# Second layer's input projections: from float32 products to three float32r products each

## Chip, cores and metric

One core of one Trainium2 chip. The metric is device time in microseconds of one execution, the median of several runs.

## What is computed

Two blocks of two layers each over 512 tokens of width 1024, in float32. The change touches the second layer of the first block, a gated linear recurrence (`c_layer` of the reference) over the 512 tokens and 256 context tokens:

```
q, zf, zb, i, g = split_cols(modulate(x, shift, scale) @ w_in, widths)
zfc, zbc, ic    = split_cols(hc @ w_in[:, C_F_WIDTH:3 * C_F_WIDTH + C_I_WIDTH], ...)
q = silu(q) * 128 ** -0.5          # 8 heads, key width 128
o_f = scan(q, i, zf), o_b = scan(q, i, zb, reversed)     # each starts from the context's state
y = rmsnorm(o_f + o_b) * g_norm * silu(g) @ w_out
x_new = layer_norm(DEEPNORM_ALPHA * x + gate * y)
```

`w_in` is 1024 x 5120. Those products with `w_in` are the input projections meant in the title.

## The kernel before

The kernel is one program per engine: PE (matmul), ACT, DVE, POOL and SP (which starts the weight loads), written out in order and joined by semaphores. Weights come in chunks of 1024 x 256 (1 MB) into three slots `WR`, used in turn; SP (L1391 on) loads chunk n once the last product of chunk n-3 has been done.

**Two ways to multiply.** Most stages split a float32 chunk into a high part (`hi`, float32r, one copy by ACT or DVE) and a low part (`lo`, the difference, one subtraction by POOL at L3011, written over the raw chunk), split the activations alike, and sum three float32r matmuls per 128 rows of the contraction: hi by hi, hi by lo, lo by hi (`split_f`, L698 to L700). The second layer's input projections multiply the raw float32 chunk by the float32 rows `HT` (`product_half`, L989, L993, L998). One such matmul stands in the trace as two instructions.

**Order of the second layer.** The projections are cut into units, each of two halves that fill one of two PSUM banks (`obank`): for every head `z` has three units (forward 512 columns, backward 512 columns, context 2 x 256), for every pair of heads `q` has two of 512 columns and `i` three of 2 x 256, and `g` has four keys of two units of 2 x 256. A first stretch makes z, q, i for the first head or pair. Then follow eight steps (`STEPS`, st = 0 to 7), one per head. In each, PE forms seven levels of attention inside blocks of 128 tokens (`levels(st, 0)` to `(st, 6)`, L1013, written `lv0` to `lv6` below) plus the chunk states, and the units needed next are put between them by hand: `c_slots` gives the number of halves in each of eight places, `between(0)` to `between(7)`. Steps 0, 2, 4 carry z of the next head and q of the next pair (5 units), steps 1, 3, 5 z and i (6 units), step 6 z and three units of g, step 7 the last five units of g.

**What a level needs.** POOL forms the arguments (`level_args`, L2998 to L3000, two level buffers `HW`, so level g waits for the matmuls of level g-2), ACT takes the exponential (`level_exp`, L1673), DVE multiplies by keys and queries (`level_operand`, L2304 and L2305), PE multiplies, DVE merges the result (`level_scores`, L2326).

**What the next step needs.** When `between(2)` has ended the third unit of z of the next head, ACT empties it (L1624) and makes keys (L1655), an exponential (L1641), the exponential for level 5, a logarithm (L1647) and the exponential for level 6, with table loads between. After the logarithm DVE runs `log_f_and_sums` (L2267, four scans L2273 to L2276, three small operations L2278 to L2280, of which L2279 reads two operands in SBUF) and signals `hg_sums`. From this wait ACT's `state_factors` (L1660 to L1669), DVE's `state_operands` (L2286) behind them, with which PE starts the next step (transposes, L1084), and POOL's arguments of the next step's first level. DVE's order is: operand 5, `log_f_and_sums`, scores 4, operand 6, scores 5, `state_operands`, scores 6.

**After the steps.** Heads are normed on DVE (L2392), turned on PE (L1049), split into hi by ACT (L1693) and lo by DVE (L2399), and multiplied by `w_out` as three float32r products (L638 to L640). ACT's order there is: hi of the first chunk `y10.0` (L1429), then hi of the heads.

The rows x stay in SBUF (`X`, L2546 adds the result to them). The tables (`TAB`) hold masks for the attention of the first and third layers.

Of the kernel before, what the change touches and what calls it, by code (L numbers as in the profile page):

```python
# [15 lines left out]
F32 = mybir.dt.float32  # L16
U32 = mybir.dt.uint32
I32 = mybir.dt.int32
ALU = mybir.AluOpType
# [29 lines left out]
def table_layout():  # L49

    sizes = [("ident", P), ("ones", P), ("pick", 2), ("win_lo", P), ("win_hi", P), ("dil", 1280),
             ("lv", P * len(LEVELS)), ("rot_ax", P), ("rot_pt", P),
             ("cos_ax", L), ("sin_ax", L), ("chunk", L), ("cols", 6)]
    at, out = 0, {}
    for name, n in sizes:
        out[name] = (at, at + n)
        at += n
    return out, at


def make_tables():
# [9 lines left out]
    put("pick", i[:, None] % 32 == np.arange(2)[None, :])  # L71
# [53 lines left out]
def program(nc, a, out, stop=99):  # L125
    lay, tw = table_layout()
    ctx = ExitStack()
    with ctx:
# [55 lines left out]
        chunks = []  # L184
# [18 lines left out]
        TAB_FIRST = lay["pick"][1]  # L203
# [5 lines left out]
        PICK = tab("pick")  # L209
# [14 lines left out]
        HKS = view(w + 19456, L, name="h_keys")  # L224
# [3 lines left out]
        HO = view(hi_at, TL, D, name="h_out")  # L228
# [9 lines left out]
        def c_slots(st):  # L238
# [8 lines left out]
            if st == LAST:  # L247
                share = (2, 2, 2, 2, 2, 0, 0, 0)
# [63 lines left out]
        Y_HI, Y_LO = parts("ab_out_hi", ht_at, KD, LT), parts("ab_out_lo", w + 4608, KD, LT)  # L312
        C_HI = parts("c_out_hi", w + 4096, KD, L)
# [224 lines left out]
        def _(pe):  # L538
# [10 lines left out]

            def chunk(pieces, kt=KD):  # L550

                n = len(chunks)
                s = n % WSLOTS
                chunks.append((pieces, kt))
                wcount[s] += 16 * len(pieces)
                pe.wait_ge(wload[s], wcount[s])
                return WR[:, s]
# [31 lines left out]
            def split_chunk(name, pieces, kt=KD, by="a"):  # L589
# [5 lines left out]
                w_hi, w_lo = OWN_HI[name] if name in OWN_HI else W_HI[:, len(splits) % 2], W_LO[n % WSLOTS]  # L595
# [4 lines left out]
                splits.append((n % WSLOTS, kt, w_hi, wload[n % WSLOTS], wcount[n % WSLOTS], by, hi_done, len(hi_list)))  # L600
# [365 lines left out]
            c_weights, c_release = {}, {}  # L966
# [6 lines left out]
            def product_half(unit, half):  # L973

                kind, key, part = unit
                if half == 0:
                    if part == 0:
                        c_weights[kind, key] = chunk(c_pieces(kind, key))
                        c_release[kind, key] = len(released)
                        released.append((None, 0))  # L980
# [4 lines left out]
                wv = c_weights[kind, key]  # L985
                ps = obank[n % 2]
                if kind in "zq" and part < 2:
# [3 lines left out]
                elif kind == "z":  # L991
                    for k in range(KD):
                        last = pe.matmul(ps[:, half * LC:(half + 1) * LC], wv[:, k, half * P:(half + 1) * P], HT[:, k, L:LT],  # L993
                                         start=k == 0, stop=k == KD - 1)
# [2166 lines left out]
```

## Time and profile before

| | |
|---|---|
| median of 3 runs | 2315.05 us (2310.82 to 2320.57) |
| profiled execution, its own time | 2313.38 us |
| its span, first to last instruction | 2311.5 us |
| mean granted clock of TensorE | 0.974 |
| PE busy | 2140.4 us (93%) |
| DVE busy | 1055.3 us (46%) |
| POOL busy | 807.8 us (35%) |
| ACT busy | 668.6 us (29%) |

PE is TensorE's matmul queue, ACT ScalarE, DVE VectorE, POOL GpSimd, SP the queue that issues loads. A timeline row gives the start and the duration in us, engine, source line, operation, output and inputs with shape, the number of instructions merged, and in brackets the idle time before it and what ended it. Matmuls overlap, so their pace is read from one start to the next and not from the duration. The granted clock is a share of TensorE's full speed.

### The profile page before, as it was taken

Reading aid. Unit: us, or ns where it says so; the run is one execution under the profiler, and the core shown is the slowest. Engines: PE = TensorE matmul, PEld = TensorE weight load, DVE = VectorE, ACT = ScalarE, POOL = GpSimd, SP = SyncE. Lnnn points to the kernel's source line nnn. Section 1 sums busy time; section 2 is a strip of 40 time slices with the busy share of each in tenths; the row PEclk is TensorE's granted clock in tenths of the full one; section 3 lists DMA queues with packets and bytes.
Section 4 is the critical chain, followed back from the end, with each engine's and each line's share of the span. In section 5 each row is a group of like instructions: output and inputs, shape, how many; then the busy total and the mean of one; then the engine's idle time right before and its main releaser. Section 6 shows DMA issues by size and latency. Waiting matters only on the chain. (4 is left out here: it accounts for less than half of the span.)

```text
span 2311.5 us, 27285 instructions
## 1 busy us (share of the span) xinstructions
PE 2140.4 (93%) x11287; PEld 1710.3 (74%) x11287; DVE 1055.3 (46%) x1685; ACT 668.6 (29%) x1043; POOL 807.8 (35%) x429
## 2 busy tenths in 40 slices
PE   4999988989999999987998889999998999999998
PEld 3887767867575767876756678888887688888886
DVE  1113674663566555559985651111126674111114
ACT  3223323324545454632102441000013443100011
POOL 1421113411333333328200025554544234554553
PEclk7999999989999999998999999999999999999999
DMA  9233123533111111121111122322322222322322
GB/s 295 69 110 97 40 71 92 128 110 91 37 37 37 37 37 37 55 82 60 37 55 37 56 73 74 109 91 91 106 79 90 91 91 74 109 91 91 106 86 82
DMA packets 183114, 187.41 MB, mean 81 GB/s; under 512 B 25728, under 2 KB 162256, under 8 KB 182864
## 3 DMA queue, kind: packets, MB, share of 16 engines
q1 hardware_dynamic: 173040, 175.42, 24.6%
q10 hardware_dynamic: 9376, 8.16, 1.3%
q8 instruction: 90, 1.47, 0.3%
q0 software_dynamic: 576, 2.10, 0.2%
q14 instruction: 32, 0.26, 0.0%
HBM read 183.56 MB, written 2.10 MB: 80 GB/s over the span
## 5 line engine op out<-in xcount | busy, mean ns | idle before, releaser
L3011 POOL TENSOR_TENSOR weights_lo<-weights_raw,weights_hi 128x2048 fp32r<-128x2048 f32 (+1 forms) x101 | 456.8, 4523 | 863.6 <-ACT weights_hi L1429 667.5
L698 PE MATMUL ring<-input_hi,weights_hi 128*128 128x512 f32 x784 | 305.5, 390 | 4.1 <-POOL weights_lo L3011 3.9
L700 PE MATMUL ring<-input_hi,weights_lo 128*128 128x512 f32 x784 | 305.1, 389 | 0.0
L699 PE MATMUL ring<-input_lo,weights_hi 128*128 128x512 f32 x784 | 305.1, 389 | 0.0
L2837 DVE CAST weights_hi<-weights_raw 128x2048 fp32r<-128x2048 f32 (+1 forms) x72 | 87.6, 1217 | 366.2 <-PE ring L700 173.9
L2998 POOL TENSOR_TENSOR h_w<-h_p 128x512 f32<-128x512 f32 x56 | 77.1, 1377 | 356.0 <-PE ring L1013 239.1
L989 PE MATMUL obank<-acts,weights_raw 128*128 128x512 f32 x384 | 175.6, 611 | 0.0
L698 PEld LDWEIGHTS ring<-input_hi,weights_hi 128*128 128x128 f32 x784 | 147.1, 188 | 36.2 <-issue 5.8
L699 PEld LDWEIGHTS ring<-input_lo,weights_hi 128*128 128x128 f32 x784 | 147.2, 188 | 30.6
L700 PEld LDWEIGHTS ring<-input_hi,weights_lo 128*128 128x128 f32 x784 | 147.2, 188 | 30.4
L998 PE MATMUL obank<-weights_raw,acts 128*128 128x256 f32 x640 | 142.1, 380 | 0.0
L1347 PE MATMUL ring<-weights_lo,hidden_hi 128*128 128x512 f32 x352 | 137.0, 389 | 0.0
L1348 PE MATMUL ring<-weights_hi,hidden_lo 128*128 128x512 f32 x352 | 137.0, 389 | 0.0
L1346 PE MATMUL ring<-weights_hi,hidden_hi 128*128 128x512 f32 x352 | 136.9, 389 | 0.0
L989 PEld LDWEIGHTS obank<-acts,weights_raw 128*128 128x128 f32 x384 | 73.8, 198 | 84.8 <-issue 84.7
L998 PEld LDWEIGHTS obank<-weights_raw,acts 128*128 128x128 f32 x640 | 119.9, 190 | 16.1 <-issue 0.8
L2858 DVE TENSOR_TENSOR f_gate<-f_gate,ring 128x1024 f32<-128x1024 f32 x22 | 26.9, 1221 | 212.4 <-PE ring L700 212.4
L3114 POOL TENSOR_TENSOR hidden_lo<-f_gate,hidden_hi 128x1024 fp32r<-128x1024 f32 x22 | 52.6, 2391 | 162.3 <-ACT hidden_hi L1925 162.3
L1925 ACT ACTIVATE hidden_hi<-f_gate 128x1024 fp32r<-128x1024 f32 x22 | 23.4, 1063 | 246.8 <-DVE f_gate L2858 246.8
L1429 ACT ACTIVATE weights_hi<-weights_raw 128x2048 fp32r<-128x2048 f32 x32 | 61.2, 1912 | 96.0 <-DMA weights_raw<-in_w_in_ab 53.3
L698 PE MATMUL ring<-ab_in_hi,weights_hi 128*128 128x512 f32 (+1 forms) x224 | 77.7, 347 | 10.4 <-POOL ab_in_lo L3017 10.4
L1013 PEld LDWEIGHTS ring<-h_w 128*128 128x128 f32 x448 | 58.4, 199 | 37.0 <-DVE h_w L2305 31.2
(465 smaller groups left out, 4391.0 us busy)
## 6 DMA issues: line engine op xcount, KB each, us to landing
weights_raw<-in_w_ada SPq DMA_DIRECT2D x24, 1024.0 KB, 5.3
weights_raw<-in_ffn_w_gate SPq DMA_DIRECT2D x22, 1024.0 KB, 5.4
weights_raw<-in_ffn_w_up SPq DMA_DIRECT2D x22, 1024.0 KB, 5.3
weights_raw<-in_ffn_w_down SPq DMA_DIRECT2D x16, 1024.0 KB, 5.0
weights_raw<-in_w_in_c SPq DMA_DIRECT2D x12, 1024.0 KB, 5.2
weights_raw<-in_w_in_ab SPq DMA_DIRECT2D x9, 1024.0 KB, 7.8
weights_raw<-in_w_in_c SPq DMA_DIRECT2D x16, 512.0 KB, 5.3
weights_raw<-in_ev_w_in SPq DMA_DIRECT2D x8, 1024.0 KB, 5.5
```

What stands on the lines that cost most here:

```text
L698: pe.matmul(o, hi[:, k, ms], xh[:, k, t0:t0 + n], start=k == 0, stop=False)
L699: pe.matmul(o, hi[:, k, ms], xl[:, k, t0:t0 + n], start=False, stop=False)
L700: last = pe.matmul(o, lo[:, k, ms], xh[:, k, t0:t0 + n], start=False, stop=k == KD - 1)
L989: last = pe.matmul(ps[:, 0:L], wv[:, k, part * P:(part + 1) * P], HT[:, k, 0:L], start=k == 0, stop=k == KD - 1)
L998: last = pe.matmul(ps[:, half * WC:(half + 1) * WC], HT[:, k, t * P:(t + 1) * P], wv[:, k, :], start=k == 0, stop=k == KD - 1)
L1346: pe.matmul(o, F_HI[f // 2][:, f % 2, ts], hi[:, k, :], start=f == 0, stop=False, skip_group_check=True)
L1347: pe.matmul(o, F_HI[f // 2][:, f % 2, ts], lo[:, k, :], start=False, stop=False, skip_group_check=True)
L1348: last = pe.matmul(o, F_LO[f // 2][:, f % 2, ts], hi[:, k, :], start=False, stop=end, skip_group_check=True)
L1429: act.activation(w_hi[:, 0:kt, :], WR[:, slot, 0:kt, :], ACT.Copy).then_inc(done, 1)
L2837: dve.tensor_copy(w_hi[:, 0:kt, :], WR[:, slot, 0:kt, :]).then_inc(done, 1)
L2998: pool.tensor_tensor(w4[:, :, :, 0, :], refs.to_broadcast([P, 2, n, h2]), p4[:, :, :, 0, :], ALU.subtract)
L3011: pool.tensor_tensor(W_LO[slot][:, 0:kt, :], WR[:, slot, 0:kt, :], w_hi[:, 0:kt, :], ALU.subtract).then_inc(sem("w_lo"), 1)
```

## The change

All of z, q, i, g but the first head's z and the first pair's q become three float32r products. Split are i0, then in pairs (z1, q1), (z2, i1), (z3, q2), (z4, i2), (z5, q3), (z6, i3), (z7, g0), then g1, g2, g3: 18 chunks (`C_SPLIT`). Chunks of even index use one raw slot, of odd index another; the third slot holds the high part of the odd ones. So a slot is loaded again only when all products of its chunk are done. ACT makes each high part (`c_weights_hi`) and POOL each low part (`c_weights_lo`), in steps 0 to 6 after level 3's and after level 6's work, in step 7 after level 2's and level 5's. The rows' high parts go where `X` and some tables were, so `X` is written to DRAM from POOL's queue and read back by SP behind the second chunk of the output product; the table for the third layer's attention is loaded later by ACT's queue. DVE makes the six high parts of the rows before `abs_z(0)` and two low parts after `log_f_and_sums(0)`, POOL the other low parts, the context's when (z, 0, 2) is done. The order of i0's three units changes. In step 7 the halves move from (2, 2, 2, 2, 2, 0, 0, 0) to (1, 1, 2, 2, 2, 2, 0, 0). `levels(st, 1)` stands ahead of the state sums before and after.

```
+        X_KEPT = nc.dram_tensor("x_kept", (TL, P, D), F32).ap()
+        x_back_after = []
...
-                share = (2, 2, 2, 2, 2, 0, 0, 0)
+                share = (1, 1, 2, 2, 2, 2, 0, 0)
...
+        C_XH, C_XH2 = parts("c_in_hi", x_at, TL, KD, P), parts("c_in_hi_ctx", own_at, 2, KD, P)
+        C_XL = parts("c_in_lo", ht_at, KD, LT)
+        C_SPLIT = [("i", 0)]
+        for hb, j in STEPS[:-1]:
+            C_SPLIT += [("z", HH * hb + j + 1), ("iq"[j == 0], hb + 1) if hb + 1 < HEADS // HH else ("g", 0)]
+        C_SPLIT = C_SPLIT[:15] + [("g", 1), ("g", 2), ("g", 3)]
...
+        def c_hi_homes(i):
+
+            if i % 2:
+                return [(0, KD, C_IN_WR[c_wr_slot[0]])]
+            return C_LATE if i >= 12 else [(0, KD, C_IN_HO)]
...
+            def c_ready(kind, key):
+
+                if (kind, key) not in C_SPLIT:
+                    c_reserve(kind, key)
+                    n = c_chunk[kind, key]
+                    pe.wait_ge(wload[slot_of[n]], arrival[n])
+                    c_raw[kind, key] = WR[:, slot_of[n]]
+                    return
+                i = C_SPLIT.index((kind, key))
+                if i:
+                    c_reserve(kind, key, slot_of[c_chunk["i", 0]] if i % 2 == 0 else c_odd_slot[0])
+                if (kind, key) == ("g", 3):
+                    holder[c_wr_slot[0]] = c_chunk["g", 3]
+                    x_back_after.append(len(chunks) + 1)
+                pe.wait_ge(sem("c_w_hi"), c_parts_made(i))
+                pe.wait_ge(sem("c_w_lo"), c_parts_made(i))
+                c_raw[kind, key] = None
...
-                if kind in "zq" and part < 2:
+                if wv is None:
+                    last = split_half(unit, half, ps)
...
+            def split_half(unit, half, ps):
+
+                kind, key, part = unit
+                i = C_SPLIT.index((kind, key))
+                lo = W_LO[slot_of[c_chunk[kind, key]]]
+                if kind in "zq" and part < 2:
+                    for k in range(KD // 2 * half, KD // 2 * (half + 1)):
+                        ms = slice(part * P, (part + 1) * P)
+                        pe.matmul(ps[:, 0:L], c_hi(i, k)[:, ms], C_XH[:, :, k, :], start=k == 0, stop=False)
+                        pe.matmul(ps[:, 0:L], c_hi(i, k)[:, ms], C_XL[:, k, 0:L], start=False, stop=False)
+                        last = pe.matmul(ps[:, 0:L], lo[:, k, ms], C_XH[:, :, k, :], start=False, stop=k == KD - 1)
+                elif kind == "z":
+                    o, ms = ps[:, half * LC:(half + 1) * LC], slice(half * P, (half + 1) * P)
+                    for k in range(KD):
+                        pe.matmul(o, c_hi(i, k)[:, ms], C_XH2[:, :, k, :], start=k == 0, stop=False)
+                        pe.matmul(o, c_hi(i, k)[:, ms], C_XL[:, k, L:LT], start=False, stop=False)
+                        last = pe.matmul(o, lo[:, k, ms], C_XH2[:, :, k, :], start=False, stop=k == KD - 1)
+                else:
+                    t = 2 * part + half
+                    o = ps[:, half * WC:(half + 1) * WC]
+                    for k in range(KD):
+                        pe.matmul(o, c_x_hi(t, k), c_hi(i, k), start=k == 0, stop=False)
+                        pe.matmul(o, c_x_hi(t, k), lo[:, k, :], start=False, stop=False)
+                        last = pe.matmul(o, C_XL[:, k, t * P:(t + 1) * P], c_hi(i, k), start=False, stop=k == KD - 1)
+                return last
...
+            pe.wait_ge(sem("c_in_lo"), 1)
+            product(("i", 0, 2))
+            c_odd_slot = [slot_of[-1]]
+            mod_next(15)
+            c_wr_slot.append(slot_of[-1])
+            c_before.append(len(chunks) - 1)
+            pe.wait_ge(sem("c_in_lo_v"), 2)
             product(("i", 0, 0))
-            mod_next(15)
+            pe.wait_ge(sem("c_in_lo"), 3)
             product(("i", 0, 1))
-            product(("i", 0, 2))
...
+                if held_before[n] is not None:
+                    sp.wait_ge(*released[held_before[n]])
...
+                if n == x_back_after[0]:
+                    for t in range(TL):
+                        sp.wait_ge(sem(f"x_kept{t}"), 16)
+                        sp.dma_start(X[:, t, :], X_KEPT[t]).then_inc(sem(f"x_back{t}"), 16)
...
+            def c_weights_hi(i):
+
+                n = c_chunk[C_SPLIT[i]]
+                for before in (c_before[:2], c_before[2:])[i] if i < 2 else (c_chunk[C_SPLIT[i - 2]],):
+                    act.wait_ge(*released[before])
+                act.wait_ge(wload[slot_of[n]], arrival[n])
+                for k0, k1, home in c_hi_homes(i):
+                    act.activation(home[:, :, :], WR[:, slot_of[n], k0:k1, :], ACT.Copy).then_inc(sem("c_w_hi"), 1)
...
             h1_tile(5)
+            c_weights_hi(0)
...
             mod_next(14)
+            take_product(("i", 0, 2))
+            mod_next(15)
+            state_factors(0)
+            c_weights_hi(1)
             take_product(("i", 0, 0))
-            state_factors(0)
             level_exp(0)
             level_exp(1)
-            mod_next(15)
             take_product(("i", 0, 1))
-            take_product(("i", 0, 2))
             mod_columns(1, 11)
...
                 level_exp(7 * st + 2)
+                if not more:
+                    c_weights_hi(2 * st + 2)
                 between(0)
                 if st == LAST:
                     s5_row_loads()
                 level_exp(7 * st + 3)
+                if more:
+                    c_weights_hi(2 * st + 2)
                 between(1)
...
                 level_exp(7 * st + 5)
                 if more:
                     log1p(st + 1)
+                else:
+                    c_weights_hi(2 * st + 3)
                 between(3)
                 level_exp(7 * st + 6)
+                if more:
+                    c_weights_hi(2 * st + 3)
                 between(4)
                 if more:
                     state_factors(st + 1)
...
+            act.dma_start(TAB[:, DIL:tw], a["tables"][:, DIL:tw]).then_inc(sem("dil_in"), 16)
...
+            for t in range(6):
+                if t < TL:
+                    dve.wait_ge(sem(f"x_kept{t}"), 16)
+                dve.wait_ge(*read_of(f"h1.{t}"))
+                home = C_XH[:, t] if t < TL else C_XH2[:, t - TL]
+                dve.tensor_copy(home, HT[:, :, t * P:(t + 1) * P]).then_inc(sem("c_in_hi"), 1)
+
+            def c_in_lo(t):
+
+                dve.wait_ge(*product_filled(("q", 0, 1)))
+                ts = slice(t * P, (t + 1) * P)
+                dve.tensor_tensor(C_XL[:, :, ts], HT[:, :, ts], C_XH[:, t], ALU.subtract).then_inc(sem("c_in_lo_v"), 1)
...
             log_f_and_sums(0)
+            c_in_lo(0)
+            c_in_lo(1)
             state_operands(0)
...
+                if c == 0:
+                    dve.wait_ge(sem(f"x_back{t}"), 16)
...
+            def c_weights_lo(i):
+
+                s = slot_of[c_chunk[C_SPLIT[i]]]
+                pool.wait_ge(sem("c_w_hi"), c_parts_made(i))
+                for k0, k1, home in c_hi_homes(i):
+                    pool.tensor_tensor(W_LO[s][:, k0:k1, :], WR[:, s, k0:k1, :], home[:, :, :], ALU.subtract).then_inc(sem("c_w_lo"), 1)
+
             if stop >= 2:
+                for t in range(TL):
+                    pool.wait_ge(sem("x1_ready"), t + 1)
+                    pool.dma_start(X_KEPT[t], X[:, t, :]).then_inc(sem(f"x_kept{t}"), 16)
+                c_weights_lo(0)
+                pool.wait_ge(sem("c_in_hi"), 6)
+                pool.wait_ge(*product_filled(("z", 0, 2)))
+                in_tiles = lambda v: v.rearrange("p k (t c) -> p t k c", c=P)
+                pool.tensor_tensor(in_tiles(C_XL[:, :, L:LT]), in_tiles(HT[:, :, L:LT]), C_XH2[:, :, :, :], ALU.subtract).then_inc(sem("c_in_lo"), 1)
+                pool.wait_ge(*product_filled(("q", 0, 1)))
+                for t in (2, 3):
+                    ts = slice(t * P, (t + 1) * P)
+                    pool.tensor_tensor(C_XL[:, :, ts], HT[:, :, ts], C_XH[:, t], ALU.subtract).then_inc(sem("c_in_lo"), 1)
                 pool.wait_ge(sem("hg_sums"), 1)
                 level_args(0)
                 level_args(1)
+                c_weights_lo(1)
                 for st in range(len(STEPS)):
                     more = st + 1 < len(STEPS)
                     for i in range(2, 7):
                         level_args(7 * st + i)
+                        if i == (3 if more else 2):
+                            c_weights_lo(2 * st + 2)
+                        if i == (6 if more else 5):
+                            c_weights_lo(2 * st + 3)
                     if st == LAST:
                         lo_upto("y10.0")
                     if more:
```

## Rows read from the trace of the kernel before

**Rows 1.** Page: busy times, two groups with mean ns, one DMA issue with us to landing

```profile
PE 2140.4 (93%) x11287; PEld 1710.3 (74%) x11287; DVE 1055.3 (46%) x1685; ACT 668.6 (29%) x1043; POOL 807.8 (35%) x429
...
L3011 POOL TENSOR_TENSOR weights_lo<-weights_raw,weights_hi 128x2048 fp32r<-128x2048 f32 (+1 forms) x101 | 456.8, 4523 | 863.6 <-ACT weights_hi L1429 667.5
...
L1429 ACT ACTIVATE weights_hi<-weights_raw 128x2048 fp32r<-128x2048 f32 x32 | 61.2, 1912 | 96.0 <-DMA weights_raw<-in_w_in_ab 53.3
...
weights_raw<-in_w_in_c SPq DMA_DIRECT2D x12, 1024.0 KB, 5.2
```

**Rows 2.** Timeline of PE, first layer: start us, us, instruction

```profile
99.73 0.39 PE L700 MATMUL ring<-ab_in_hi,weights_lo 128*128 128x512 f32 x1
...
106.08 0.28 PE L698 MATMUL ring<-ab_in_hi,weights_hi 128*128 128x256 f32 x1
...
107.03 0.28 PE L700 MATMUL ring<-ab_in_hi,weights_lo 128*128 128x256 f32 x1
```

**Rows 3.** Timeline of PE, step 3 of the second layer

```profile
745.03 7.03 PE L989 MATMUL obank<-acts,weights_raw 128*128 128x512 f32 x16
751.90 1.05 PE L1013 MATMUL ring<-h_w 128*128 128x128 f32 x8
752.79 7.07 PE L993 MATMUL obank<-acts,weights_raw 128*128 128x256 f32 x32
759.70 1.05 PE L1013 MATMUL ring<-h_w 128*128 128x128 f32 x8
...
778.54 1.16 PE L1013 MATMUL ring<-h_w 128*128 128x128 f32 x8 [1.12 <-DVE h_w L2305]
...
787.54 1.06 PE L1013 MATMUL ring<-h_w 128*128 128x128 f32 x8
```

**Rows 4.** Timeline of PE, step 4

```profile
816.86 1.05 PE L1013 MATMUL ring<-h_w 128*128 128x128 f32 x8
...
826.52 2.08 PE L1013 MATMUL ring<-h_w 128*128 128x128 f32 x8 [3.31 <-DVE h_w L2305]
828.39 8.62 PE L989 MATMUL obank<-acts,weights_raw 128*128 128x512 f32 x16
836.84 1.05 PE L1013 MATMUL ring<-h_w 128*128 128x128 f32 x8
...
843.13 1.16 PE L1013 MATMUL ring<-h_w 128*128 128x128 f32 x8 [0.70 <-DVE h_w L2305]
```

**Rows 5.** Table by stretches, six us of step 4 (granted clock before the DMA share)

```profile
826.00:832.00 6.00, 5.48 (x13) 3.41 (x14) 5.25 (x6) 3.48 (x3) 0.00 (x0) 0.54 0.00 0
```

**Rows 6.** Timeline of ACT, step 3

```profile
768.40 1.58 ACT L1647 ACTIVATE h_t<-h_t,tables 128x1536 f32<-128x1536 f32 x1
...
771.29 1.06 ACT L1673 ACTIVATE h_w<-h_w 128x1024 f32<-128x1024 f32 x1
```

**Rows 7.** Timeline of DVE, step 3

```profile
774.64 0.66 DVE L2276 TENSOR_TENSOR_SCAN h_p<-h_t,tables 128x255 f32<-128x255 f32 x1
...
775.42 0.16 DVE L2279 TENSOR_TENSOR small<-h_p,h_t 128x6 f32<-128x6 f32 x1
```

**Rows 8.** Timeline of DVE, last mixer: two scans over the same size

```profile
1855.63 1.23 DVE L2960 TENSOR_TENSOR_SCAN r_xc<-r_a,r_gi 128x512 f32<-128x512 f32 x1
...
1857.62 5.50 DVE L2960 TENSOR_TENSOR_SCAN r_xc<-r_a,r_gi 128x512 f32<-128x512 f32 x1
```

**Rows 9.** Timeline of POOL in the same stretch

```profile
1857.26 4.77 POOL L3011 TENSOR_TENSOR weights_lo<-weights_raw,weights_hi 128x2048 fp32r<-128x2048 f32 x1 [19.64 <-ACT weights_hi L1429]
```

**Rows 10.** Timeline of DVE, after the second layer's steps

```profile
1042.41 4.58 DVE L2470 SCALAR_TENSOR_TENSOR s_par<-s_par 128x16 f32<-128x16 f32 x1
```

**Rows 11.** Timeline of DVE, start of the second layer

```profile
529.34 1.76 DVE L2260 SCALAR_TENSOR_TENSOR h_t<-h_z 128x1536 f32<-128x1536 f32 x1 [12.63 <-ACT h_z L1624]
```

**Rows 12.** Timeline of PE, end of the second layer

```profile
1005.42 1.10 PE L1049 MATMUL ring<-tables,h_out 128*128 128x128 f32 x8
...
1018.28 0.77 PE L638 MATMUL ring<-c_weights_hi,c_out_hi 128*128 128x512 f32 x1 [1.08 <-DVE c_out_lo L2399]
```

More of the change, by code:

```diff
@@ L548, in take, with reserve, chunk @@
                 return ring[n % 3]
-            def chunk(pieces, kt=KD):
+            def reserve(pieces, kt=KD, slot=None):
                 n = len(chunks)
-                s = n % WSLOTS
+                s = next_slot[0] if slot is None else slot
+                next_slot[0] = (s + 1) % WSLOTS
                 chunks.append((pieces, kt))
                 wcount[s] += 16 * len(pieces)
-                pe.wait_ge(wload[s], wcount[s])
-                return WR[:, s]
+                slot_of.append(s)
+                arrival.append(wcount[s])
+                held_before.append(holder.get(s))
+                holder[s] = n
+                return n
+            def chunk(pieces, kt=KD):
+                n = reserve(pieces, kt)
+                pe.wait_ge(wload[slot_of[n]], arrival[n])
+                return WR[:, slot_of[n]]
             def used_with_unit():
@@ L976, in product_half @@
                 if half == 0:
[L977 to L980, printed above, removed]
+                    if (kind, key) not in c_raw:
+                        c_ready(kind, key)
                     n = products[unit] = len(products)
@@ L984, in product_half @@
                 n = products[unit]
-                wv = c_weights[kind, key]
+                wv = c_raw[kind, key]
                 ps = obank[n % 2]
-                if kind in "zq" and part < 2:
+                if wv is None:
+                    last = split_half(unit, half, ps)
+                elif part < 2:
                     for k in range(KD // 2 * half, KD // 2 * (half + 1)):
@@ L990, in product_half @@
                                          start=k == 0, stop=k == KD - 1)
-                elif kind == "z":
+                else:
                     for k in range(KD):
                         last = pe.matmul(ps[:, half * LC:(half + 1) * LC], wv[:, k, half * P:(half + 1) * P], HT[:, k, L:LT],
-                                         start=k == 0, stop=k == KD - 1)
-                else:
-                    t = 2 * part + half
-                    for k in range(KD):
-                        last = pe.matmul(ps[:, half * WC:(half + 1) * WC], HT[:, k, t * P:(t + 1) * P], wv[:, k, :],
                                          start=k == 0, stop=k == KD - 1)
@@ L1002, in product_half @@
                 last.then_inc(sem("products_filled"), 1)
-                if part == C_PARTS[kind] - 1:
+                c_left[kind, key] -= 1
+                if c_left[kind, key] == 0:
                     released[c_release[kind, key]] = (sem("products_filled"), n + 1)
+            def split_half(unit, half, ps):
[22 more added lines that the diff above has]
+                return last
             def levels(st, i):
```

65 lines of the change are left out of this document (42 added, 23 removed).

## Prediction

> **What bounds the kernel now.** I read the busy shares first: PE works 2140 of 2311.5 us [rows 1]. In the changed stretch, from the first projections to the output product at 1018.28, I then read PE's timeline step by step. PE runs almost without a gap up to T, the end of the third unit of z, at which level 3 starts (759.70 in step 3, 816.86 in step 4) [rows 3, 4]. After T a chain on ACT and DVE paces it: level 6 starts at T + 18.84 in step 3 after 1.12 us of waiting; in step 4 PE waits 3.31 us before level 5 [rows 3, 4]. That chain runs from T through ACT's logarithm, done at 769.98, to DVE's scans [rows 6, 7]. So PE is the bound before T, and a second chain is within 1 to 4 us of it behind T.
>
> **What the products save.** In the first layer 28 float32r matmuls of 512 columns start in 106.08 - 99.73 = 6.35 us, 0.227 each, and 8 of 256 columns in 0.95 us, 0.119 each [rows 2]. A unit of 512 columns takes 751.90 - 745.03 = 6.87 us now and 24 x 0.227 = 5.44 then; a unit of 2 x 256 takes 6.91 and 48 x 0.119 = 5.70 [rows 3]. That is 1.43 and 1.21 us less. Split are 14 + 6 = 20 units of the first kind (z, q) and 7 + 12 + 8 = 27 of the second (z context, i, g): 28.6 + 32.7 = 61 us of PE's time. Were PE the bound throughout, the execution would take 2313.4 - 61 = 2252 us.
>
> The Trainium skill (FP8 and Floating Point Precision, TensorE Precision Notes) says that true FP32 takes four passes through the array. Read with one pass per float32r product, it would save a quarter of the 324 us of these units, 81 us, and end at 2232 us. The starts above give 61, and I use them.
>
> **What splitting costs, where it is covered.** Each of 18 chunks costs ACT 1.91 us and POOL 4.52 us (group means) [rows 1]. The first pair of a step comes between the work of levels 3 and 4. Its slot was free since the end of the step before, loads land after 5.2 us [rows 1], and the product wants it only behind level 3. ACT idles there. I cost it at nothing; its cover is the two z units on PE, and if it went, up to 4.5 us per step would show. The second pair is the z chunk of the next step, whose slot is freed at T. The load lands about T + 6, ACT copies it after the exponential for level 6, at 771.29 + 1.06 = T + 12.65 [rows 6], so until T + 14.6, and then POOL subtracts until about T + 19.5. PE wants it after the next level 0: no wait by itself.
>
> **What POOL's subtraction does to DVE.** This is the step that decides. A scan on DVE issued 0.36 us after such a subtraction of 4.77 us took 5.50 us, and 1.23 us when free; it ended only after the subtraction [rows 8, 9]. Even an operation of 16 columns took 4.58 us [rows 10]. DVE operations with two operands in SBUF stop for the whole of POOL's instruction. In step 3 the fourth scan starts at 774.64 = T + 14.94 and L2279, also with two operands in SBUF, at 775.42 [rows 7]. The new subtraction asks at T + 14.6, while the third scan runs, and is next. Were it 0.5 us later the fourth scan would pass and L2279 would be held, so small shifts don't help. `hg_sums` moves by what is left of the subtraction, about 4.4 us. Queued behind it on DVE are operand 6 and `state_operands`, on ACT `state_factors`, on POOL the next arguments. Late next is PE's level 6 and level 0 of the next step.
>
> The Trainium skill (SBUF — State Buffer, Who interferes with whom) has the rule: a DVE instruction with two SBUF inputs contends with a GpSimd one that reads SBUF, and the later one fully blocks. The trace agrees, 5.50 against 1.23 us.
>
> **The steps.** Before T each of steps 0 to 6 saves 2 x 1.43 + 1.21 = 4.07 us. After T:
> - Steps with q (three): level 0 of the next step starts at T + 26.27 now (843.13), bound by DVE [rows 4]. With the chain 4.4 later it starts at T + 30.7. Net +0.3.
> - Steps with i or g (four): level 6 starts at T + 18.84 + 4.4 = 23.2. PE has then waited about 7 us. After 3.31 us of waiting in step 4 the granted clock was 0.54, half speed, 1.2 GHz [rows 5]; level 5 took 2.08 for 1.05 and the units 8.62 for 7.03, a loss of 2.6 us [rows 4]. Level 6 (1.0), one unit (5.70), the transposes (1.1) and 2.6 make T + 33.6 against T + 27.84 now [rows 3]. Net 5.8 - 4.1 = +1.7.
>
> Sum of the steps: 0.9 + 6.8 = +8 us. Without the clock it would be 0.9 - 4 x 0.9 = -3.
>
> **The start.** The context's low part starts on POOL when (z, 0, 2) ends, 0.8 us before `abs_z(0)` starts now [rows 11], and holds it 3.7 us; I let half reach the chain, since the keys fill part of it on ACT. Two more POOL parts and DVE's own two (1.2 us each, from 1.76 for 1536 columns [rows 11]) stand before i0's latent units, so PE waits some 5 us and loses clock. Less 3 x 1.21 saved: I take +5. Bounds: -4 (all covered) and +9 (nothing). DVE's six high parts (0.6 to 1.2 us each) lie in 12.63 us of idle time [rows 11]; writing and reading x (4 x 0.5 MB each way) lies beside other work, at most +2. The reordered tables and the late table load: 0, covered by the whole layer in between.
>
> **Step 7 and the output product.** Five units save 6.1 us. But g3's slot is freed only with g1, and its high and low part follow level 5's exponential and arguments: about 4 us of waiting and 2.6 of clock, so 0. The chunk y10.0 gets the third slot only after g's last product, just ahead of the first turn of heads. Load 5.2, copy 1.9, subtraction 4.5: 11.6 [rows 1]. Today 12.9 us lie between that turn and the product (1005.42 to 1018.28) [rows 12]. But ACT's copies of the heads are queued behind y10.0's copy, and the norm of the third pair on DVE (two operands in SBUF) waits for the subtraction's end; behind it come 2.2 us of norm, the turn and the split, some 19 us. I take +6; bounds 0 and +9.
>
> **Sum.** 8 + 5 + 0 + 6 = +19 against this execution's own 2313.4: 2332. The median of the runs shown lies 1.7 us above it, so 2334 us.
>
> **Rivals.**
> - *The hold misses the chain.* If DVE gets `hg_sums` out before POOL's subtraction, the steps keep nearly all of 4.1 us: about 3 x 4.1 + 4 x 3.5 = 26 us less, with the start and the end still +3: 2292. For it: ACT's copy could wait for a late load. Against: rows 7, 8 and 10, and a load of 5.2 us where 12 are there. With nothing held at the ends either, 2284. Chance 0.20.
> - *PE stays the bound throughout*, the full count: 2254 with the median's offset. Against: PE waits for DVE already. Chance 0.03.
> - *It cancels.* The chain is late as I say, but PE's clock stays up or half of the hold is covered: steps -3, start +2, end +3: 2317. Chance 0.22.
> - *Slower*, my forecast: its mechanism is the port held from T + 14.6, its price 4.4 us per step, and it decides once that exceeds the 4.07 saved before T. Chance 0.55; its own range is 2327 to 2352.
>
> A difference of 0.5%, 11.6 us, is about what can be told from none here. Chances: faster 0.23, same 0.22, slower 0.55. The range, 2286 to 2350, takes in the first and third rival and the bounds.
>
> **What would show it.** Fourth scan or L2279 at 4 to 5 us in each of seven steps; level 6 at about T + 23; units of z at 5.44 us; a granted clock near 0.5 behind level 6; `y10.0`'s subtraction ending after the turns. If the scans keep 0.66 us and level 6 stays at T + 19, the forecast is wrong.

## The result, and the profile after

The changed kernel takes 2338.0 us (2335.4 to 2338.3, three runs) against 2315.05: a ratio of 1.0093, 95% interval 1.0066 to 1.0121. It is slower, by 23 us; 2334 was forecast. The mean granted clock of TensorE is 0.962, and the span of the profiled execution 2336.2 us, 24.7 more than before.

The page after, to be read against [rows 1]: busy shares, then one group of instructions (busy us, mean ns | idle before, releaser).

```profile
PE 2100.3 (90%) x11879; PEld 1751.5 (75%) x11879; DVE 1134.2 (49%) x1693; ACT 699.0 (30%) x1062; POOL 920.6 (39%) x457
...
L1103 PE MATMUL ring<-h_w 128*128 128x128 f32 x448 | 70.9, 308 | 67.3 <-DVE h_w L2438 67.3
```

PE is busy 40 us less than before, yet the span is longer. GpSimd's subtractions in the other stages keep their mean of 4.52 us. The second row says where the time went: PE waits 67.3 us for `h_w`, the operands of the levels that DVE writes. The same group had 23.0 us before.

PE's timeline in step 3, then in step 4, against [rows 3] and [rows 4]. T is the second row of the first fence and the first of the second.

```profile
742.30 1.16 PE L1103 MATMUL ring<-h_w 128*128 128x128 f32 x8 [0.29 <-DVE h_w L2438]
...
767.77 1.06 PE L1103 MATMUL ring<-h_w 128*128 128x128 f32 x8
...
790.92 2.07 PE L1103 MATMUL ring<-h_w 128*128 128x128 f32 x8 [6.58 <-DVE h_w L2438]
...
800.13 1.06 PE L1103 MATMUL ring<-h_w 128*128 128x128 f32 x8
```

```profile
825.51 1.06 PE L1103 MATMUL ring<-h_w 128*128 128x128 f32 x8
...
848.68 2.08 PE L1103 MATMUL ring<-h_w 128*128 128x128 f32 x8 [5.35 <-DVE h_w L2438]
...
856.11 1.16 PE L1103 MATMUL ring<-h_w 128*128 128x128 f32 x8 [0.82 <-DVE h_w L2438]
```

In step 3 level 6 starts at 790.92 = T + 23.15 (before T + 18.84), behind 6.58 us of idle time, takes 2.07 us instead of 1.16, and level 0 of the next step starts at T + 32.36 (before T + 27.84). In step 4 it is T + 23.17 and T + 30.60 (before T + 20.0 and T + 26.27).

Who is late is on DVE; its rows of step 3, which answer to [rows 7], then POOL's in the same stretch:

```profile
781.61 1.19 DVE L2408 TENSOR_TENSOR_SCAN h_p<-h_t,tables 128x511 f32<-128x511 f32 x1
782.73 4.96 DVE L2409 TENSOR_TENSOR_SCAN h_p<-h_t,tables 128x255 f32<-128x255 f32 x1
...
788.00 0.17 DVE L2413 COPY small<-small 128x12 f32<-128x12 f32 x1
...
789.77 1.09 DVE L2438 TENSOR_TENSOR h_w<-h_w,h_q 128x512 f32<-128x512 f32 x1
```

```profile
782.32 4.82 POOL L3172 TENSOR_TENSOR weights_lo<-weights_raw,c_w_hi 128x2048 fp32r<-128x2048 f32 x1 [5.48 <-ACT c_w_hi L1745]
```

The third scan takes 1.19 us. The fourth, over 255 columns, starts 0.41 us after POOL's subtraction (L3172) and ends 0.55 us after it: 4.96 us against 0.66. It is so in each of steps 0 to 6 (4.95 to 5.00 us). The state sums (L2413) and with them ACT's `small` (L1770, which waited 5.49 us for them) and DVE's operands of level 6 (L2438) come that much later.

The clock in the 3.2 us behind that wait, by stretches (duration, then busy us and instructions of PE, PEld, DVE, ACT, POOL, the granted clock, DMA share, GB/s):

```profile
790.90:794.10 3.20, 3.18 (x15) 3.18 (x16) 1.98 (x2) 3.12 (x8) 1.47 (x2) 0.51 0.00 0
```

0.51 is the lower of the clock's two levels, 1.2 GHz; PE had been idle for 6.58 us.

Where the 24.7 us of span lie, by marks on PE in both traces:

| stretch | before | after | difference | forecast |
|---|---|---|---|---|
| first instruction to z's first product | 497.90 | 502.66 | +4.8 | 0 |
| z's first product to level 0 of step 0 | 64.89 | 68.20 | +3.3 | +5 |
| steps 0 to 6, level 0 to T, sum | 204.43 | 178.36 | -26.1 | -28.5 |
| steps 0 to 6, T to next level 0, sum | 190.22 | 224.33 | +34.1 | +36.5 |
| level 0 of step 7 to its level 6 | 48.91 | 53.35 | +4.4 | 0 |
| level 6 of step 7 to first output product | 11.93 | 18.17 | +6.2 | +6 |
| rest | | | -2.1 | 0 |

The first row can't be told from scatter, and I don't count it as the change's: the two kernels of the experiments that have the first layer of the kernel before start z's first product at 497.48 and 503.44, and those with that of the changed kernel at 500.61 to 506.94. The two rows of step 7 together are +10.7, 60.84 us before and 71.52 after.

### The profile page after: what moved, and what is told of

It reads as the page before. It is cut to its first block and busy times, and to the rows that moved or that the text cites. A ratio compares the mean times of both kernels' runs of the same rounds, so it can differ in the third digit from the quotient of the medians.

```text
span 2336.2 us, 28558 instructions
## 1 busy us (share of the span) xinstructions
PE 2100.3 (90%) x11879; PEld 1751.5 (75%) x11879; DVE 1134.2 (49%) x1693; ACT 699.0 (30%) x1062; POOL 920.6 (39%) x457
## 5 line engine op out<-in xcount | busy, mean ns | idle before, releaser
L3136 POOL TENSOR_TENSOR h_w<-h_p 128x512 f32<-128x512 f32 x56 | 85.4, 1524 | 141.9 <-PE ring L1103 128.3
L1103 PE MATMUL ring<-h_w 128*128 128x128 f32 x448 | 70.9, 308 | 67.3 <-DVE h_w L2438 67.3
L1103 PEld LDWEIGHTS ring<-h_w 128*128 128x128 f32 x448 | 63.2, 216 | 74.5 <-DVE h_w L2438 73.6
L1783 ACT ACTIVATE h_w<-h_w 128x1024 f32<-128x1024 f32 x56 | 58.6, 1055 | 105.3 <-POOL h_w L3138 105.1
L2437 DVE TENSOR_TENSOR h_w<-h_w,h_k 128x512 f32<-128x512 f32 x56 | 65.1, 1162 | 48.4 <-ACT h_w L1783 47.8
L2043 ACT ACTIVATE f_gate<-ring 128x1024 f32<-128x1024 f32 x22 | 22.7, 1031 | 183.8 <-PE ring L742 173.8
```

Of the source, the lines that this page charges most:

```text
L1103: last = pe.matmul(ps[:, cs], W[:, 0, cs], W[:, 1, cs], start=True, stop=True)
L2437: dve.tensor_tensor(ws, ws, keys, ALU.mult)
L3136: pool.tensor_tensor(w4[:, :, :, 0, :], refs.to_broadcast([P, 2, n, h2]), p4[:, :, :, 0, :], ALU.subtract)
```

## Experiments

Each is compared with runs of the kernel before on the same chip (2315.2 to 2316.9 us).

**1. The low part behind the next arguments.** GpSimd's order in steps 0 to 6, in the changed kernel:

```
-                        if i == (6 if more else 5):
+                        if i == 5 and not more:
                             c_weights_lo(2 * st + 3)
...
                         level_args(7 * st + 7)
+                        c_weights_lo(2 * st + 3)
                         level_args(7 * st + 8)
```

> The changed kernel with one order on GpSimd turned round: the low part of the next z chunk is made after the arguments of the next step's level 0, not ahead of the wait for the state sums. ScalarE's rounding of the same chunk stays where it was. T is the end of the step's third z unit. Theory (GpSimd's 4.8 us subtraction at T+14.6 holds VectorE's fourth scan): the fourth scan goes back from 4.96 to about 0.7 us, level 6 starts at about T+18.8 instead of T+23.2, and because the subtraction then falls on the operands of the next level 0, the next level 0 starts at about T+28.4 instead of T+32.4; with seven such steps 2338 - 28 = 2310 us (2304 to 2322). Rival (ScalarE's 1.9 us rounding in its queue is what delays the sums): nothing moves, 2338 within 4, and the fourth scan may be short while level 6 still starts past T+22.

Measured: 2319.7 us, ratio to the kernel before 1.0020 (1.0008 to 1.0033). DVE in step 3 (T is 763.23 here), then POOL:

```profile
778.19 0.66 DVE L2409 TENSOR_TENSOR_SCAN h_p<-h_t,tables 128x255 f32<-128x255 f32 x1
...
783.89 4.75 DVE L2419 TENSOR_TENSOR h_z<-h_z,h_k 128x1536 f32<-128x1536 f32 x1 [1.21 <-ACT h_t L1779]
```

```profile
782.47 4.56 POOL L3172 TENSOR_TENSOR weights_lo<-weights_raw,c_w_hi 128x2048 fp32r<-128x2048 f32 x1
```

The fourth scan takes 0.66 us, level 6 starts at T + 18.85, the next level 0 at T + 28.2. ACT's rounding was not touched, so the rival falls. The hold has not gone but moved: `state_operands` (L2419) starts inside POOL's subtraction, takes 4.75 us for 1.76 and ends 1.6 us after it. The gain is 18 us, not 28. I took 4 us from every step, but the three steps with q had only 2.6 us between their T + 30.6 and this kernel's T + 28.0. In step 6 the chunk is g1, which PE wants right behind level 6, and it waited 3.83 us for the low part: nothing gained there. And the moved hold makes PE wait 2.7 us for `state_operands` (L2419) ahead of level 0 of steps 1, 3 and 5; from level 0 to level 1 the granted clock is then 0.82, 0.95 and 0.74, and T comes 1.9, 0.4 and 3.0 us later after level 0 than in the changed kernel.

**2. DVE makes the low part.** GpSimd's call in steps 0 to 6 goes, PE waits for DVE's semaphore in its place, and DVE gets:

```
                 level_operand(7 * st + 6)
+                if more:
+                    s = slot_of[c_chunk[C_SPLIT[2 * st + 3]]]
+                    dve.wait_ge(sem("c_w_hi"), c_parts_made(2 * st + 3))
+                    dve.tensor_tensor(W_LO[s][:, :, :], WR[:, s, :, :], C_IN_WR[c_wr_slot[0]][:, :, :],
+                                      ALU.subtract).then_inc(sem("c_w_lo_v"), 1)
                 level_scores(st, 5)
```

> The changed kernel with the low part of the z chunks of steps 0 to 6 made by VectorE, behind the operands of level 6, in place of GpSimd. Theory (the shared hold, not the amount of work): VectorE pays about 2.3 us per step for it, off the chain to level 6; the scans are short again, level 6 starts at T+18.8, the next level 0 at T+26 to T+27; 5 to 6 us per step, 2338 - 38 = 2300 us (2294 to 2314), faster than the kernel before. Rival (VectorE is what bounds the step, so 2.3 us more work on it costs about what the hold cost): 2325 to 2338.

Measured: 2306.9 us, ratio 0.9962 (0.9948 to 0.9976): 31 us less than the changed kernel and 8 less than the kernel before. DVE in step 3, and PE there:

```profile
770.35 0.67 DVE L2413 TENSOR_TENSOR_SCAN h_p<-h_t,tables 128x255 f32<-128x255 f32 x1
...
774.12 2.71 DVE L2587 TENSOR_TENSOR weights_lo<-weights_raw,c_w_hi 128x2048 fp32r<-128x2048 f32 x1
```

```profile
755.39 1.06 PE L1107 MATMUL ring<-h_w 128*128 128x128 f32 x8
...
774.25 1.16 PE L1107 MATMUL ring<-h_w 128*128 128x128 f32 x8 [2.30 <-DVE h_w L2442]
...
782.01 1.06 PE L1107 MATMUL ring<-h_w 128*128 128x128 f32 x8
```

The same subtraction costs DVE 2.71 us, POOL 4.8 us. T to level 6 is 18.86 us, T to the next level 0 26.62. Steps 0 to 6 take 370.7 us against 402.7. It is not the amount of work on DVE that bounds the step: with 2.7 us more of it per step the kernel is faster, and the scans, which GpSimd's instruction no longer stops, take 0.67 us again.

**3. The hold alone, in the kernel before.** Nothing of the change but a subtraction on constants, in steps 1 to 6:

```
+                    if more and st:
+                        pool.wait_ge(sem("hg_wexp"), 7 * st + 7)
+                        one = lambda n: IDENT.unsqueeze(1).to_broadcast([P, n, P])
+                        pool.tensor_tensor(view(w + 19456, 12, P, name="spare"), one(12), one(12), ALU.subtract)
+                        pool.tensor_tensor(view(bc_at + 1536, 4, P, name="spare2"), one(4), one(4), ALU.subtract)
                     if more:
                         pool.wait_ge(sem("hg_sums"), st + 2)
```

> The kernel before, with nothing of the change but GpSimd's 2048 element subtraction (two instructions, on constants, into spare memory, read by nobody) in steps 1 to 6, after the exponentials of level 6, ahead of the wait for the state sums. It has no ScalarE copy, no third product, no other order. Theory (the hold alone costs the chain 4 us per step): the scans of those steps end at about T+17 to T+19 instead of T+15.3, level 6 waits 4 to 6 us and the clock falls as it does in the changed kernel: 2315 + 20 to 34 = 2335 to 2349. Rival (the cost is in the order of ScalarE and in the new levels, the hold is hidden behind TensorE): 2315 within 4.

Measured: 2342.5 us, ratio 1.0125 (1.0100 to 1.0150), 27 us more. DVE, then POOL and PE, in step 3:

```profile
787.89 3.17 DVE L2274 TENSOR_TENSOR_SCAN h_p<-tables,h_t 128x256 f32<-128x256 f32 x1
790.98 1.99 DVE L2275 TENSOR_TENSOR_SCAN h_p<-h_t,tables 128x511 f32<-128x511 f32 x1
```

```profile
787.37 3.14 POOL L3042 TENSOR_TENSOR spare<-tables 128x1536 f32<-128x1536 f32 x1 [3.67 <-ACT h_w L1673]
790.48 1.42 POOL L3043 TENSOR_TENSOR spare<-tables 128x512 f32<-128x512 f32 x1
```

```profile
774.64 1.05 PE L1013 MATMUL ring<-h_w 128*128 128x128 f32 x8
...
796.78 2.07 PE L1013 MATMUL ring<-h_w 128*128 128x128 f32 x8 [4.42 <-DVE h_w L2305]
...
807.16 1.06 PE L1013 MATMUL ring<-h_w 128*128 128x128 f32 x8
```

The second scan waits out the first of the two instructions (3.17 us for 0.67), the third what is left of the second (1.99 for 1.20). Level 6 waits 4.42 us and takes 2.07. From level 0 of step 0 to level 0 of step 7 the kernel takes 422.6 us for 394.65. So two instructions whose results nobody reads, beside a kernel with nothing of the three products in it, cost more than the whole change does.

**4. The same instruction in another place.** The two `pool.tensor_tensor` lines of experiment 3, without the wait, between `level_args(7 * st + 7)` and `level_args(7 * st + 8)`, again in steps 1 to 6.

> The kernel before with the same added 2048 element subtraction on GpSimd in steps 1 to 6, but behind the arguments of the next step's level 0 in place of ahead of the wait for the state sums: the same work, another place. Theory (it is the place, the scans, that costs): the scans are short as in the kernel before, level 6 starts at T+18.8 to T+20, and what the hold now falls on (keys and states, operands of the next level 0) is nearly hidden behind the units that follow level 6: 2315 + 0 to 8 = 2319 us. Rival (any 4.6 us of GpSimd per step costs the same): 2340 like the run with the early place.

Measured: 2319.2 us, ratio 1.0019 (1.0009 to 1.0030): 4 us for what cost 27 in the other place. The scans take 1.22, 0.66, 1.20 and 0.66 us again. POOL's two instructions in step 3, and DVE's row beside them:

```profile
778.91 2.74 POOL L3045 TENSOR_TENSOR spare<-tables 128x1536 f32<-128x1536 f32 x1
781.61 2.55 POOL L3046 TENSOR_TENSOR spare<-tables 128x512 f32<-128x512 f32 x1
```

```profile
780.34 2.92 DVE L2286 TENSOR_TENSOR h_z<-h_z,h_k 128x1536 f32<-128x1536 f32 x1 [1.23 <-ACT h_t L1669]
```

`state_operands` (L2286) waits out the first of them, 2.92 us where it takes 1.76 alone. The second, of 512 columns, asks while L2286 runs and takes 2.55 us, where it took 1.42 in experiment 3: the stop works in both directions, the same in all six steps.

**5. The clock.** Products for nothing, ahead of PE's wait for level 6:

```
+                if i == 6 and st < LAST:
+                    ps = take(f"lv{st}.{i}", "v")
+                    for k in range(16):
+                        pe.matmul(ps[:, 0:L], c_x_hi(0, k % KD), C_XH[:, :, k % KD, :], start=True, stop=True)
+                    pe.wait_ge(sem("hg_w"), 7 * st + i + 1)
```

> The changed kernel with 16 dummy float32r products of 512 columns (3.6 us, into the bank that level 6 then overwrites) ahead of TensorE's wait for the operands of level 6 in steps 0 to 6. Theory (of the cost of a step, 1.7 to 2.6 us are the granted clock that falls in the wait): level 6 takes 1.1 us instead of 2.07 and the unit after it runs at the full clock; in the steps with i or g units 1.5 to 2 us each, in the q steps nothing, 2338 - 7 = 2331 us (2327 to 2335). Rival (what follows level 6 is set by VectorE's next operands, so the clock is hidden): 2338 within 3.

Measured: 2337.3 us, ratio to the kernel before 1.0106 (1.0079 to 1.0133): not to be told from the changed kernel. The profiled execution shows why. PE in step 3, and the stretch from level 0 of that step to its level 1 (columns as above):

```profile
792.93 1.16 PE L1109 MATMUL ring<-h_w 128*128 128x128 f32 x8 [2.99 <-DVE h_w L2444]
...
800.70 1.06 PE L1109 MATMUL ring<-h_w 128*128 128x128 f32 x8
```

```profile
742.60:754.00 11.40, 11.34 (x62) 9.97 (x63) 4.15 (x8) 5.56 (x7) 2.43 (x3) 0.85 0.09 32
```

Level 6 runs in 1.16 us, and level 0 of the next step starts at T + 31.0 in steps 3 and 5 instead of T + 32.4 and T + 33.4. But behind the 2.15 us that PE then waits for level 0 of steps 1 and 3, the granted clock averages 0.85, and the way to T is 1.6 us longer there. Behind the same wait of 2.16 us in step 5 the clock stays at 1.00. The seven steps take 400.6 us for 402.7. The clock's loss is real (1.4 to 2.4 us in three steps with i or g, as the fourth, step 1, still lost it), but what the fill gives back is lost at other waits. In step 7, where nothing was filled, PE waits 3.98 us for `h_scores` where the changed kernel waits 2.74, the granted clock averages 0.75 over the 13.6 us from level 1 to level 2, and T comes 28.5 us after level 0 for 25.0.

**6. The output chunk's slot.**

```
                     x_back_after.append(len(chunks) + 1)
+                    next_slot[0] = slot_of[c_chunk["i", 0]]
```

> The changed kernel with one load in another slot: the first chunk of the output weights goes to the slot that the second last gate chunk leaves, not to the one that holds the last gate chunk's rounded half, so it can be loaded a unit or two earlier. Theory (part of the 10.7 us that the end costs is ScalarE waiting for this transfer, 5.25 us at 1031.7): its rounding no longer waits, the rounding of heads 0 and 1 and all behind it come 4 to 6 us earlier, the first output product at about 1040 instead of 1045: 2338 - 5 = 2333 us (2330 to 2336). Rival (the heads wait for VectorE's normed heads anyway, or the load is slowed by the transfers beside it): 2338 within 2.

Measured: 2331.2 us, ratio to the kernel before 1.0076 (1.0061 to 1.0091), 6.8 us less than the changed kernel. First the changed kernel's rows of step 7 and behind it on ACT, DVE, POOL and PE, then this kernel's on ACT and PE:

```profile
1031.71 1.91 ACT L1530 ACTIVATE c_weights_hi<-weights_raw 128x2048 fp32r<-128x2048 f32 x1 [5.25 <-DMA weights_raw<-in_w_out_c]
```

```profile
980.93 3.47 DVE L2500 TENSOR_TENSOR h_sq<-h_out 128x512 f32<-128x512 f32 x1
```

```profile
980.42 5.11 POOL L3172 TENSOR_TENSOR weights_lo<-weights_raw,c_w_hi_late 128x1536 fp32r<-128x1536 f32 x2 [3.47 <-ACT c_w_hi_late L1745]
...
1005.72 5.24 POOL L3172 TENSOR_TENSOR weights_lo<-weights_raw,c_w_hi 128x2048 fp32r<-128x2048 f32 x1 [2.97 <-ACT c_w_hi L1745]
```

```profile
986.03 1.13 PE L1205 MATMUL ring<-h_q,tables 128*128 128x128 f32 x8 [2.74 <-DVE h_scores L2459]
...
1011.06 0.55 PE L1091 MATMUL obank<-c_w_hi,c_in_hi 128*128 128x256 f32 x1 [4.79 <-issue]
...
1026.90 1.06 PE L1103 MATMUL ring<-h_w 128*128 128x128 f32 x8
...
1045.07 0.47 PE L680 MATMUL ring<-c_weights_hi,c_out_hi 128*128 128x512 f32 x1 [1.39 <-DVE c_out_lo L2532]
```

```profile
1022.97 1.90 ACT L1531 ACTIVATE c_weights_hi<-weights_raw 128x2048 fp32r<-128x2048 f32 x1
```

```profile
1036.32 0.77 PE L680 MATMUL ring<-c_weights_hi,c_out_hi 128*128 128x512 f32 x1 [1.09 <-DVE c_out_lo L2533]
```

The wait of 5.25 us for `in_w_out_c` is gone, and from level 0 of step 7 to the first output product it is 66.1 us for 71.5. All of this gain lies behind level 6 (1026.90 in the changed kernel): from there it is 12.8 us, where the changed kernel has 18.2 and the kernel before 11.9. The way from level 0 to level 6 is untouched, 53.3 us.

**7. The start.** DVE makes the context's low part, behind `abs_z(0)`, and POOL's part of the latents waits for the state sums:

```
-                pool.tensor_tensor(in_tiles(C_XL[:, :, L:LT]), in_tiles(HT[:, :, L:LT]), C_XH2[:, :, :, :],
-                                   ALU.subtract).then_inc(sem("c_in_lo"), 1)
                 pool.wait_ge(*product_filled(("q", 0, 1)))
+                pool.wait_ge(sem("hg_sums"), 1)
...
             abs_z(0)
+            dve.wait_ge(sem("c_in_hi"), 6)
+            dve.tensor_tensor(in_tiles(C_XL[:, :, L:LT]), in_tiles(HT[:, :, L:LT]), C_XH2[:, :, :, :],
+                              ALU.subtract).then_inc(sem("c_in_lo_ctx"), 1)
             log_f_and_sums(0)
```

> The changed kernel with the start of the stage arranged round the port: the context's low part is made by VectorE behind abs z instead of GpSimd beside it, and GpSimd's two latent tiles wait for the state sums. Theory (the start's 3.3 us are again VectorE held: abs z took 5.64 us): abs z takes 1.76 us, the state sums come at about 546 instead of 550, TensorE's wait of 5.2 us ahead of the i units shrinks to about 2, and level 0 of step 0 comes 3 us earlier: 2338 - 3 = 2335 us (2332 to 2337). Rival (the latents' low parts, now later, take the place of the wait): 2338 within 1.5.

Measured: 2337.3 us, ratio 1.0091 (1.0069 to 1.0113), 0.7 us less than the changed kernel, which is within the scatter. The changed kernel's rows on DVE, POOL and PE, then this kernel's on DVE and POOL:

```profile
533.44 5.64 DVE L2393 SCALAR_TENSOR_TENSOR h_t<-h_z 128x1536 f32<-128x1536 f32 x1 [9.02 <-ACT h_z L1725]
...
550.14 3.20 DVE L2385 TENSOR_TENSOR c_in_lo<-acts,c_in_hi 128x1024 fp32r<-128x1024 f32 x2
```

```profile
532.92 4.54 POOL L3182 TENSOR_TENSOR c_in_lo<-acts,c_in_hi_ctx 128x2048 fp32r<-128x2048 f32 x1 [4.13 <-PE obank L1061]
```

```profile
553.39 0.58 PE L1091 MATMUL obank<-c_w_hi_early,c_in_hi 128*128 128x256 f32 x1 [5.20 <-DVE c_in_lo L2385]
```

```profile
535.81 1.76 DVE L2393 SCALAR_TENSOR_TENSOR h_t<-h_z 128x1536 f32<-128x1536 f32 x1 [9.02 <-ACT h_z L1725]
537.49 2.28 DVE L2541 TENSOR_TENSOR c_in_lo<-acts,c_in_hi_ctx 128x2048 fp32r<-128x2048 f32 x1
...
550.13 4.51 DVE L2385 TENSOR_TENSOR c_in_lo<-acts,c_in_hi 128x1024 fp32r<-128x1024 f32 x2
```

```profile
550.37 6.50 POOL L3186 TENSOR_TENSOR c_in_lo<-acts,c_in_hi 128x1024 fp32r<-128x1024 f32 x2 [19.21 <-DVE small L2413]
```

`abs_z` takes 1.76 us again, and from it to level 0 of step 0 are 35.6 us, where the changed kernel has 37.4 and the kernel before 33.45: 1.9 of the 4 us come back. For the rest the rival's rows stand: the latents' parts of both engines now meet, 4.51 us on DVE for 3.20 and 6.50 on POOL for the 4.74 of the changed kernel.

**8. Experiments 2, 6 and 7 together.**

> The three edits together: VectorE makes the low parts of the z chunks of steps 0 to 6, the first output chunk has the earlier slot, and the start is arranged round the port. They touch different stretches, so if each acts as said they add: 2306.9 - 5 - 3 = 2299 us (2295 to 2303), against 2315 of the kernel before. Rival (what one frees the next wait takes back): 2303 to 2307.

Measured: 2302.9 us, ratio 0.9949 (0.9935 to 0.9964). That is 12 us ahead of the kernel before and 35 ahead of the changed one, with nothing left out. Of 8 us expected beyond experiment 2, 4 came; in the profiled executions the start gives 1.5 (from `abs_z(0)` to level 0 of step 0) and the end 4.75 (from level 0 of step 7 to the first output product).

**9. Two products in place of three.** Left out of every split unit is the product with the inputs' low part, for example:

```
                         pe.matmul(ps[:, 0:L], c_hi(i, k)[:, ms], C_XH[:, :, k, :], start=k == 0, stop=False)
-                        pe.matmul(ps[:, 0:L], c_hi(i, k)[:, ms], C_XL[:, k, 0:L], start=False, stop=False)
                         last = pe.matmul(ps[:, 0:L], lo[:, k, ms], C_XH[:, :, k, :], start=False, stop=k == KD - 1)
```

> The changed kernel without the product of the rounded weights with the inputs' low part: every split unit has two float32r products in place of three, so it leaves out the correction for the rounding of the inputs. Nothing else moves. Theory (TensorE sets the way from level 0 to T, the end of the third z unit; from T on the chain over the state sums does, and it is tied to T): a unit falls from 5.44 to about 3.7 us and T comes 4 to 5.5 us earlier after level 0 in steps 0 to 6, while level 6 stays at T+23 and the next level 0 loses only what followed level 6 on TensorE: 2338 - 35 = 2303 us (2292 to 2312). Rival 1 (TensorE bound all along): some 37 units by 1.8 us, 2338 - 66 = 2272 us. Rival 2 (the chain of level operands bounds the first half as well): 2325 to 2338.

Measured: 2301.5 us, ratio 0.9936 (0.9919 to 0.9953). PE in step 3, from its level 0 over T (749.05) and level 6 to the next level 0:

```profile
728.01 1.16 PE L1100 MATMUL ring<-h_w 128*128 128x128 f32 x8 [1.97 <-DVE h_w L2435]
...
749.05 1.13 PE L1100 MATMUL ring<-h_w 128*128 128x128 f32 x8 [0.97 <-DVE h_w L2435]
...
773.83 2.08 PE L1100 MATMUL ring<-h_w 128*128 128x128 f32 x8 [8.06 <-DVE h_w L2435]
...
781.71 1.06 PE L1100 MATMUL ring<-h_w 128*128 128x128 f32 x8
```

Level 0 to T falls from 25.5 to 21.0 us; T to level 6 does not, it is 24.8 us (23.15 in the changed kernel), and PE idles through 8.06 of them. Of the 5.5 us of work taken away before T, 4.4 come, as level 3 now waits 0.97 us for DVE. So PE sets the first half of a step and the chain over the sums the second, in the changed kernel too. The expectation counted 37 units, but 47 are split, so some 87 us of PE's work are taken away (20 by 1.8 and 27 by 1.9); 36.5 us reach the end.

## Why the prediction was right

**The products** hold by their pace: before T a step saves 3.94 to 3.99 us in steps 1 to 6 (4.07 forecast), and 2.3 in step 0, where the granted clock is 0.83 between levels 0 and 1 (1.00 before), behind a wait of 1.97 us that both kernels have. The Trainium skill's four passes (FP8 and Floating Point Precision, TensorE Precision Notes), read as one per float32r product, would save 5.2 us before each T; the trace does not agree.

**The hold** is the step that decided, and it is shown from four sides: the row of 4.96 us; the time coming back when it is moved or given to DVE (experiments 1 and 2); the time lost when it alone is added (3); and little lost in another place (4). Level 6 at T + 23.2 was forecast, T + 23.15 came. The trace agrees with the rule of the Trainium skill (SBUF — State Buffer, Who interferes with whom), and with its sentence that the order of issue decides who blocks: 4.96 us for 0.66 on DVE.

**Next level 0:** T + 30.7 for the steps with q was forecast, T + 30.60 to 30.68 came. For those with i or g it was T + 33.6, and 33.3, 32.4, 33.4 and 33.4 came: the clock's loss was taken a little high. Sum of the steps +8 forecast, +8.04 measured. That the sum is exact is partly luck: the saving before T and the loss after it are both 2.4 us smaller than forecast.

**The start** cost 3.3 us of the +5. Its mechanism, `abs_z` stopped by POOL (5.64 us for 1.76) and PE waiting 5.20 us for DVE's low part, stands in the rows of experiment 7.

**The end** cost 10.7 us, not 6, above the bound of 9 that I gave. The output product's term was right: from level 6 to the first output product it is 6.2 us more, for 6, and experiment 6 shows that the late load is 5.4 of them. The term that was mis-sized is step 7, which I put at 0 and which cost 4.4. The saving of 6.1 us, the wait for g3 (4.79 us at 1011.06, until POOL's low part of 1005.72 has ended) and the clock behind it (the g unit that follows takes 8.12 us for 5.99) were counted, the last two at 4 and 2.6 us. Not counted was one more hold: POOL's low part of g2 stops DVE's L2500 (980.93, 3.47 us for 0.69), `h_scores` comes late, and PE waits 2.74 us for it at 986.03, where the kernel before does not wait. No run took that hold away alone. The norm that I had named (the third pair, behind POOL's low part of `y10.0`) does stop, 4.12 us for 2.19, but in the kernel before it takes the same 4.12. The second pair's, beside g3's low part, takes 7.17 us, but it is done at 1014.45 and PE then works on without a wait until level 6 has run.

**The whole.** The changed stretch costs 22.0 us in the two traces, for 19 forecast. That the sum is so near is in part luck too: the start came 1.7 us under its term and step 7 4.4 over.

**The rivals.** PE as the bound throughout (2254) falls by experiment 9. The cancelling case rested on the clock staying up or on half of the hold being covered. Neither came: the granted clock was 0.51 behind the wait for level 6, and level 6 was 4.3 us later after T in step 3. Experiment 5 shows that filling the wait alone would not have brought it. The hold missing the chain is what experiment 2 makes of it: the steps take 24.0 us less than in the kernel before (370.7 for 394.65), where that rival had 26, but the start costs 3.6 (from `abs_z(0)` to level 0 of step 0) and the end 13.8 (74.6 for 60.84) in place of 3 together, so it ends at 2307 and not at 2292. In that end step 7 reaches T 3.4 us later than in the changed kernel (28.4 us for 25.0): PE waits 3.79 us for `h_scores`, and the granted clock averages 0.75 from level 1 to level 2.

## What to carry to other kernels

When work is split over engines, look not only at whether the engine is free but at who runs beside it: a 4.6 us elementwise instruction of GpSimd with its operands in SBUF can stop VectorE's whole chain for its length, and one order line decides whether this costs 27 us or 4. Before such an instruction is placed, list VectorE's operations on the critical chain in its window; where VectorE has room, let it do the work itself, as it needs 2.3 to 2.7 us for the same 2048 columns. And a saving on the busiest engine is worth only what lies in stretches where that engine ends last.

## What the runs showed that was not expected

- The stop works both ways, where I had counted it one way only: GpSimd's 512 columns took 2.55 us behind VectorE's 1536 column product and 1.42 in the other place (experiments 3 and 4).
- A clock kept up through one wait was lost at the next, of only 2.15 us (granted 0.85 over the 11.4 us behind it, experiment 5), in steps 1 and 3; behind the same wait in step 5 it stayed at 1.00. So the cost of such a wait has to be read case by case.
- In step 7 a norm on VectorE was stopped for 5 us and no wait of TensorE followed, since it had work up to its turn; a product of 512 columns was stopped for 2.8 us, and TensorE waited 2.74.
- Profiled executions whose first layer is the same code differ by 6 us at its end (497.48 and 503.44). A term of a few us must be read between marks within the changed stretch.
